# A two-block transformer forward pass on one core: the second attention's order of work rearranged around its recurrent and normalising pieces

## The reference, cut to what matters

```
z   = rms_norm(x, norm_mix) @ w_in
y_a = rg_lru_mixer(...)      # recurrence
y_b = short_conv_mixer(...)  # bg * causal_dwconv(cg * xs, conv_w)
y_c = fox_mixer(...)         # 4 heads of causal attention with a decay
y_d = nsa_mixer(...)         # 4 heads: selected, window and compressed keys, gated
x   = x + concat(rms_norm each) @ w_out
x   = x + (silu(gu[:, :F]) * gu[:, F:]) @ w_down
```

```
r, i  = sigmoid(xc @ w_r + b_r), sigmoid(xc @ w_i + b_i)
log_a = -8 * softplus(-lam) * r
a     = exp(log_a)
b     = sqrt(-expm1(2 * log_a)) * (i * xc)
h[t]  = a[t] * h[t-1] + b[t]
y_a   = h * gelu(gate)
```

## Time and profile before

| what | us |
|---|---|
| median of 3 runs | 774.54 (774.17 to 776.04) |
| the profiled execution, its own time | 776.68 |
| span from its first to its last instruction | 774.9 |
| PE busy | 740.8 (96%) |
| DVE busy | 551.4 (71%) |
| ACT busy | 450.1 (58%) |

### The profile page before, as it was taken

One profiled execution on the slowest core, in us unless ns is written; L12 is line 12 of the kernel. 1 busy time (PEld: TensorE's weight loads), 2 busy tenths in 40 slices (PEclk: granted clock), 3 DMA queues, 4 the chain that ended last, 5 costly groups with the idle time before them and its releaser, 6 DMA issues.

```text
span 774.9 us, 14050 instructions
## 1 busy us (share of the span) xinstructions
PE 740.8 (96%) x4998; PEld 667.2 (86%) x4998; DVE 551.4 (71%) x1064; ACT 450.1 (58%) x855; POOL 63.9 (8%) x94
## 2 busy tenths in 40 slices
PE   3999999999999999999999999979899999999998
PEld 2799888899999899999999998868698888888886
DVE  4886359898897766666666787667776877777674
ACT  5667466665655654554545766378766555554542
POOL 8001020000455000000000002000000000000000
PEclk9799999999999999999999999989999999999999
DMA  8997997888796566665666476422153766666631
GB/s 287 353 265 247 189 239 218 269 265 283 243 311 201 153 201 180 198 189 166 195 188 178 99 207 174 143 82 83 55 163 98 230 202 192 174 188 193 187 108 54
DMA packets 187220, 148.23 MB, mean 191 GB/s; under 512 B 13694, under 2 KB 171328, under 8 KB 187160
## 3 DMA queue, kind: packets, MB, share of 16 engines
q1 hardware_dynamic: 183296, 143.61, 62.8%
q10 hardware_dynamic: 2232, 3.03, 2.2%
q0 software_dynamic: 1648, 1.00, 0.6%
HBM read 146.29 MB, written 1.36 MB: 191 GB/s over the span
## 4 chain that ended last, share of the span: by engine, by line
PE 84%; ACT 5%; DVE 5%; issue 2%; DMA 2%; POOL 0%; SPq 0%; ACTq 0%; DVEq 0%; POOLq 0%
PE ps L2273 20%; PE ps L1886 14%; PE ps L1888 14%; PE ps L1887 14%; PE ps L2275 10%; DMA raw<-in_w_ada 2%; ACT w_hi L707 2%; DVE w_lo L1211 1%; DVE arena L1269 1%; PE ps L2250 1%; PE ps L2366 1%; PE ps L2141 1%; PE ps L1934 1%; PE ps L2163 1%; PE ps L2128 1%
## 5 line engine op out<-in xcount | busy, mean ns | idle before, releaser
L1211 DVE TENSOR_TENSOR w_lo<-raw,w_hi 128x1024 fp32r<-128x1024 f32 (+3 forms) x223 | 269.1, 1228 | 73.9 <-ACT w_hi L707 72.6
L2273 PE MATMUL ps<-h,w_hi 128*128 128x512 f32 x672 | 239.2, 396 | 0.0
L707 ACT ACTIVATE w_hi<-raw 128x1024 fp32r<-128x1024 f32 (+3 forms) x223 | 226.1, 1038 | 21.3 <-PE ps L1888 7.9
L2275 PE MATMUL ps<-h,w_lo 128*128 128x256 f32 x672 | 189.4, 282 | 0.0
L2273 PEld LDWEIGHTS ps<-h,w_hi 128*128 128x128 f32 x672 | 126.3, 188 | 29.6
L1886 PE MATMUL ps<-h,w_hi 128*128 128x256 f32 (+1 forms) x440 | 127.7, 290 | 2.7 <-ACT bias L1102 1.1
L2275 PEld LDWEIGHTS ps<-h,w_lo 128*128 128x128 f32 x672 | 126.2, 188 | 1.0
L1888 PE MATMUL ps<-h,w_lo 128*128 128x256 f32 (+1 forms) x440 | 124.4, 283 | 0.0
L1887 PE MATMUL ps<-h,w_hi 128*128 128x256 f32 (+1 forms) x440 | 124.4, 283 | 0.0
L1886 PEld LDWEIGHTS ps<-h,w_hi 128*128 128x128 f32 (+1 forms) x440 | 83.7, 190 | 7.7 <-issue 5.8
L1887 PEld LDWEIGHTS ps<-h,w_hi 128*128 128x128 f32 (+1 forms) x440 | 83.8, 191 | 0.0
(11 more groups left out here) (372 smaller groups left out, 1273.7 us busy)
## 6 DMA issues: line engine op xcount, KB each, us to landing
raw<-in_w_in SPq DMA_DIRECT2D x53, 512.0 KB, 5.7
raw<-in_w_down SPq DMA_DIRECT2D x44, 512.0 KB, 4.3
raw<-in_w_gate_up SPq DMA_DIRECT2D x44, 512.0 KB, 4.7
raw<-in_w_ada SPq DMA_DIRECT2D x32, 512.0 KB, 4.8
raw<-in_w_gate SPq DMA_DIRECT2D x22, 512.0 KB, 3.9
raw<-in_w_up SPq DMA_DIRECT2D x22, 512.0 KB, 5.1
raw<-in_w_ada SPq DMA_DIRECT2D x32, 256.0 KB, 6.5
raw<-in_w_o SPq DMA_DIRECT2D x8, 512.0 KB, 5.1
```

The costliest lines, as they stand in the source:

```text
L707: A(w_hi[:, m % HL, 0:w], raw[:, n % RAW, 0:w], ACT.Copy).then_inc(hi_done, 1)
L1211: V.tensor_tensor(w_lo[:, m % HL, 0:w], raw[:, n % RAW, 0:w], w_hi[:, m % HL, 0:w].bitcast(f32), sub).then_inc(lo_done, 1)
L2273: T.matmul(bank[:, :], hi, h2[:, k, :, :].rearrange("p a b -> p (a b)"), start=(k == 0), stop=False, skip_group_check=True)
L2275: ins = T.matmul(bank[:, 0:SEQ], lo, h_hi[:, k, :], start=False, stop=(k == KC - 1), skip_group_check=True)
```

## The change

On every engine the same work is done; only its order changes, and ACT needs one change of table less.

1. ACT does `exps` of the first pair before the LRU's `tanh` and `exp`.
2. DVE computes `decay_rates` in feed-forward network 1, after `hidden(2)`, and no longer between the key norms and the first scores.
3. DVE normalises the first pair before it splits the next weight panel; its wait for `gate2_ready` comes after both.
4. DVE's `lru_w` moves from round 5 to round 4, and the two `conv` calls of rounds 5 and 6 move behind the `probabilities` of the same round.
5. ACT's square root for the LRU (`lru_sqrt`) moves from round 6 to round 4, beside `y_root(0)`; the GELU moves from round 5 to after round 7.
6. PE does the compressed key's norm matmul before the LRU's gate matmuls.

```diff
 ACT
-            line.settle()
+            for g in PAIRS[0]:
+                exps(g)
+            act.wait_ge(s("lru_sig"), 4)
             act.wait_ge(s("lru_c"), 1)
             for c in range(2):
                 line(A(yT[:, c, :], ra[:, c, :], ACT.Tanh, scale=spt[7][:, c:c + 1]), "lru_tanh")
             for c in range(2):
                 line(A(ra[:, c, :], ra[:, c, :], ACT.Exp, scale=spt[6][:, c:c + 1]), "lru_a")
-            for g in PAIRS[0]:
-                exps(g)
             fill(EARLY)
...
                 if x == 4:
                     y_root(0)
-                    line(A(warm, eps_c, ACT.Exp))
-                if x == 5:
-                    line(A(lg, lg, ACT.Gelu_apprx_tanh), "lg_ready")
-                    line.settle()
-                    line(A(warm, eps_c, ACT.Exp))
-                if x == 6:
                     act.wait_ge(s("lru_w"), 1)
                     line(A(yT[:, 0:2, :], yT[:, 0:2, :], ACT.Sqrt), "lru_sqrt")
+                    line(A(warm, eps_c, ACT.Exp))
+            line(A(lg, lg, ACT.Gelu_apprx_tanh), "lg_ready")
             act.wait_ge(s("yb_ready"), 1)
             y_square(1)
+            line(A(warm, eps_c, ACT.Sqrt))
             pair_copy(*PAIRS[-1])
             y_root(1)
 DVE
                     hidden(j, 0, [e + 3 * j - 1 + k for k in range(3)])
+                if f == 0:
+                    decay_rates()
                 with dve.Fori(0, ITER) as i:
...
-            decay_rates()
             dve.wait_ge(s("kc_rms"), 1)
...
-            dve.wait_ge(s("gate2_ready"), 1)
             for g in PAIRS[0]:
                 scores(g)
-            split.ahead(nth("fill", EARLY))
             for g in PAIRS[0]:
                 probabilities(g)
+            split.ahead(nth("fill", EARLY))
+            dve.wait_ge(s("gate2_ready"), 1)
             for x, (a, b) in enumerate(PAIRS):
                 if more:
                     scores(a + 2)
                     scores(b + 2)
+                if x == 4:
+                    dve.wait_ge(s("lru_tanh"), 2)
+                    dve.wait_ge(s("lru_a2"), 1)
+                    line(stt(out=yT[:, 0:2, :], in0=xc, scalar=1.0, in1=yT[:, 0:2, :], op0=add, op1=mult), "lru_w")
...
-                if x == 5:
-                    dve.wait_ge(s("lru_tanh"), 2)
-                    dve.wait_ge(s("lru_a2"), 1)
-                    line(stt(out=yT[:, 0:2, :], in0=xc, scalar=1.0, in1=yT[:, 0:2, :], op0=add, op1=mult), "lru_w")
+                if more:
+                    probabilities(a + 2)
+                    probabilities(b + 2)
+                if x == 6:
+                    y_low(0)
                 if x in (5, 6):
...
                     conv(s_c[:, c, :], sx, 3, "sc_conv_w_2", None, c)
-                if more:
-                    probabilities(a + 2)
-                    probabilities(b + 2)
-                if x == 6:
-                    y_low(0)
 PE
+            pe.wait_ge(s("kc_sq"), 1)
+            line(T.matmul(ps[7][:, 304:304 + NCMP], half1[:, :], kcq[:, 0:NCMP], start=True, stop=True), "cmp_mm")
             arrived(pe, "in_lw")
             pe.wait_ge(s("xc_ready"), 2)
             for q in range(4):
...
                 line(T.matmul(lin(l, SEQ, SEQ * c), lw[:, g, c, :], xc[:, c, :], start=True, stop=True), "lru_mm")
-            pe.wait_ge(s("kc_sq"), 1)
-            line(T.matmul(ps[7][:, 304:304 + NCMP], half1[:, :], kcq[:, 0:NCMP], start=True, stop=True), "cmp_mm")
```

More of the change, by code:

```diff
@@ L1103, in _ @@
                        bias=vcol("lru_b_gates_2", q)), "lru_sig")
-            line.settle()
-            act.wait_ge(s("lru_c"), 1)
-            for c in range(2):
-                line(A(yT[:, c, :], ra[:, c, :], ACT.Tanh, scale=spt[7][:, c:c + 1]), "lru_tanh")
-            for c in range(2):
-                line(A(ra[:, c, :], ra[:, c, :], ACT.Exp, scale=spt[6][:, c:c + 1]), "lru_a")
             def y_square(n):
@@ L1130, in _ @@
                 exps(g)
+            act.wait_ge(s("lru_sig"), 4)
+            act.wait_ge(s("lru_c"), 1)
+            for c in range(2):
+                line(A(yT[:, c, :], ra[:, c, :], ACT.Tanh, scale=spt[7][:, c:c + 1]), "lru_tanh")
+            for c in range(2):
+                line(A(ra[:, c, :], ra[:, c, :], ACT.Exp, scale=spt[6][:, c:c + 1]), "lru_a")
             fill(EARLY)
@@ L1501, in _, with decay_rates @@
             modulate(5)
+            def decay_rates():
+                dve.wait_ge(s("lam_exp"), 1)
+                e_, s_, s2, acc_, t_ = spt[0], spt[1], spt[2], spt[3], spt[4]
+                line(V.tensor_scalar(t_, e_, 2.0, None, add))
+                line.settle()
+                line(V.reciprocal(t_, t_))
+                line.settle()
+                line(V.tensor_tensor(s_, e_, t_, mult))
+                line.settle()
+                line(V.tensor_tensor(s2, s_, s_, mult))
+                line(V.memset(acc_, 1.0 / 15))
+                for k in (13, 11, 9, 7, 5, 3, 1):
+                    line.settle()
+                    line(V.tensor_tensor(acc_, acc_, s2, mult))
+                    line.settle()
+                    line(V.tensor_scalar(acc_, acc_, 1.0 / k, None, add))
+                line.settle()
+                line(stt(out=acc_, in0=acc_, scalar=2.0, in1=s_, op0=mult, op1=mult))
+                line.settle()
+                line(V.tensor_scalar(t_, vcol("lru_lambda_2", 0, 2), -1.0, 0.0, mult, ALU.max))
+                line.settle()
+                line(V.tensor_tensor(acc_, acc_, t_, add))
+                line.settle()
+                line(V.tensor_scalar(spt[7], acc_, 8.0, None, mult))
+                line(V.tensor_scalar(spt[6], acc_, -8.0, None, mult), "lru_c")
             def raw_low(c):
```

25 lines of the change are left out of this document (removed).

## The result

The changed kernel takes 769.34 us (median of 5 runs, 768.3 to 771.58), the kernel before 776.04 beside it (5 runs, 774.17 to 777.95): the ratio on record is 0.9933, with an interval of 0.9913 to 0.9953 (the two medians alone would give 0.9914), so it is faster, by less than 1%. The profiled execution took 769.34 us with a span of 767.5, against 776.68 and 774.9.

A forecast was written before the change was run, and what follows sets the result against it. PE, busy 740.8 of 774.9 us, was taken as the bound, leaving its waits and low-clock stretches to win. Terms 5.2 + 0.7 + 0.7 + 0.3 = 6.9 us took the median from 774.54 to 767.6, range 765.4 to 770.8.

The forecast's parts named there:

- rival 1: Whole kernel: the forecast itself holds, 765.6 to 769.3 us; chance 0.72.
- start, up to turn 2: Start of the attention: first waits shrink and the clock stays full, so turn 1 comes 5.2 us earlier.
- rounds, up to turn 6: Rounds 4 to 6: both waits before turn 6 go, round 5's gather wait grows to 1.6; net 0.7 us won.
- round 7, up to the panel: Round 7: 0.7 of PE's 2.4 us of waits go, 1.7 stay.
- behind round 7, to the end: After round 7: 0.3 us won, taken between clock falling as before (nothing won) and clock full (0.7 won).
- "1.85 us": Between turn 0 and turn 1 on PE: 7.15 against 5.30 us, the difference of 1.85 charged to the low clock.
- Rival 2: Start gives half back: the gather's new wait nears 3 us or the clock falls again; 770.1 us, chance 0.13.
- that sign of the prediction: Start of the attention: PE has no wait before the first chunk, the 1.13 us there gone.
- Decay rates: Moved to feed-forward network 1 on DVE: cost 0, its next step 3.5 us late, hidden by a four-panel lead.
- Rival 3: Table loads hold ACT longer than their rows show; one less gives 1.3 us more, 766.3 or lower; chance 0.06.
- Rival 4: Tail: rounds come earlier but PE waits for late y_total(1) and second group's root; 773 to 775 us, chance 0.05.
- Rival 5: First rounds: PE's clock stays at 0.50, up to 5.3 us more per round, kernel slower, 777.5 us; chance 0.04.

The follow-up runs named there:

- e1: Changed kernel with the reordering of rounds 4 to 7 on ACT and DVE undone, only the attention's start kept changed: 771.79 us, 0.9926 of the kernel before.
- e12: Changed kernel with the compressed key's norm matmul back behind the LRU's gate matmuls on PE: 771.05 us, 0.9952 of the kernel before.
- e9: The changed kernel run and profiled again, no edit: 771.83 us, 0.9964 of the kernel before.
- e14: The kernel before, profiled again without edit (second of three repeats): 777.0 us.
- e15: The kernel before, profiled again without edit (third of three repeats): 772.43 us.
- e13: The kernel before, profiled again without edit (first of three repeats): 778.33 us.
- e16: The changed kernel, profiled once more without edit: 771.43 us.
- e2: Kernel before with only the reordering of rounds 4 to 7 applied, the attention's start as before: 775.61 us, 0.9971 of the kernel before.
- e5: Changed kernel with DVE's decay rates back ahead of the key norm, before the first scores: 771.97 us, 0.9944 of the kernel before.
- e6: Changed kernel with DVE's two convolutions back ahead of the probabilities in rounds 5 and 6: 772.16 us, 0.995 of the kernel before.
- e7: Changed kernel with ACT's GELU back in round 5, with its wait and table reload: 770.69 us, 0.9936 of the kernel before.
- e8: Changed kernel with three unread matmuls added on PE where it waits in round 7: 770.89 us, 0.9942 of the kernel before.
- e10: Changed kernel with the LRU's tanh and exp on ACT moved to round 1, behind its splits: 768.72 us, 0.9916 of the kernel before.
- e11: As e10, plus in round 6 DVE does P7's probabilities and y_low(0) before the split: 770.22 us, 0.9942 of the kernel before.
- e3: Changed kernel with ACT's first-pair exponentials back behind the LRU's tanh and exp: 771.61 us, 0.9923 of the kernel before.
- e4: Changed kernel with DVE splitting the next weight panel before normalising the first pair again: 775.21 us, 0.9977 of the kernel before.

## Why the prediction was right, and where it was not

The direction and the mechanism were right. The size was right between the two first profiles, and too large as a statement on the kernels. Over the executions timed beside e1 to e12, the kernel before has a mean of 776.04 us (70 executions); the changed kernel has 771.39 (17, of the result and e9): 4.6 less, not 6.9. That the two first profiles differ by 6.8 is luck: the terms were read from an execution of the kernel before that was dearer than two of the other three, and were compared with the cheapest of three of the changed kernel. The ratio of 6.9 us, 0.9910, lies just beyond the interval of the result, and the median of 769.34 just above the 765.6 to 769.3 of rival 1, though inside the wider range. The forecast of 767.6 also started from a median of 3 runs that lay 1.5 below the mean of the 70.

The table compares the terms with the stretch between the first profiles and with the means of all profiled executions (4 of before, 3 of the changed kernel), each a difference of two columns of the table above:

```
term                         forecast   first profiles   means
start, up to turn 2               5.2             5.15    3.75
rounds, up to turn 6              0.7             0.48    0.48
round 7, up to the panel          0.7             1.22    1.23
behind round 7, to the end        0.3            -0.06   -1.21
sum                               6.9             6.79    4.25
```

The profiles of before are four and lie 5.5 us apart, so the mean of 4.25 has a standard error of about 1.5. Steadier is what lies behind turn 1: to the end it is 257.6 us before and 257.5 after in the mean of the profiles. The gain that holds comes ahead of turn 1.

**Start.** A failed step: the term of 5.2 is too large by some 1.5. It charged "1.85 us" to the clock between turn 0 and turn 1, and took the wait of 4.60 and the root's wait of 1.41 as the kernel's. All three are one execution's. In e14 and e15 the waits are 3.0 and 0.54, that round takes 22.55 - 16.91 = 5.6 us, and turn 1 comes 2.4 earlier than in the first profile: 0.86 through ACT's root, since its matmul stands behind gate matmuls at low clock, and 7.15 - 5.64 = 1.51 through the round at low clock. The other 0.3 of the 1.85 stays at full clock, as the second head's transposes still wait for DVE. The sentence beside it, "this takes the clock to be full there, as the new wait is less than half of the old one", fails as an argument: the clock was full behind 3.0 us of standing still in e14, low behind the same 3.0 us in e13 (there the round takes 28.05 - 20.02 = 8.0 us) and low behind 1.80 in e16. e2 is a second case of low behind 3.0. The length of the wait alone does not decide it. Rival 2 named this cost and gave it to one case in eight; it is present in one of the three profiles of the changed kernel, e16, where turn 1 to turn 2 takes 6.3 us instead of 5.3.

The rest of the walk held. On the clock of the kernel before (0.61 later) turn 0 stands at 503.57, for 503.6; the scores of P1 at 506.63, for 506.7; turn 1 at 510.96, for 510.9; a new wait of 1.65, for 1.7, released by `ptb`, L895. Two things inside it were off. The new wait for the second head (0.3) was not there. And the 1.4 us by which the sigmoids were to come earlier hold only against the first profile, with its gate matmuls at low clock; with these at full clock part 6 is worth 0.5 (e12). The first chunk had no wait in two profiles of three because PE was held up in the gate matmuls by the low clock; in e16, where it was not, 1.03 is left. So that sign of the prediction came true by luck.

**Decay rates.** Cost nothing, as forecast: PE does not wait anywhere in feed-forward network 1. On DVE the first addition behind them stands here,

```profile
278.06 0.41 DVE L1548 TENSOR_TENSOR arena<-arena,ps 128x256 f32<-128x256 f32 x1
```

10.97 us behind its like of the step before (267.09), where it was 7.55 (275.42 behind 267.87): 3.4 later, for 3.5, and well inside the lead of four panels. e5 shows that they did not have to go: in their old place they end 0.3 us ahead of the first scores, in a profile without a loss against e16.

**Rounds 5 to 7.** The wait before the gather of round 5 grew to 1.35, for 1.6, both waits before turn 6 are gone, and 1.06 + 0.67 = 1.7 stay in round 7, for 1.7. Both terms together were 1.4 and are 1.7. In the table the term of round 7 is 1.2 for 0.7; 0.3 of this is the wait of turn 6's second head, which falls behind the start of turn 6. The convolution behind the probabilities is worth 1.4 of the 1.7 by itself (e6 against e5). The GELU's new place is worth 0.3 at turn 7 (e7), and nothing at the end.

**Behind round 7.** The term that failed altogether: 0.3 won was forecast, 1.2 are lost in the mean. Its local working was right: `y_total(1)` is ready 1.1 us ahead of PE, as forecast, in this row of DVE against PE's 550.94;

```profile
549.43 0.43 DVE L1703 TENSOR_TENSOR sq<-sq 128x256 f32<-128x256 f32 x1 [0.19 <-ACT sq L1108]
```

and where the clock stays full PE waits 0.43 to 0.53 for it, for 0.6 (e7, e8). But the forecast's "if the clock falls there as before" took the earlier trace rows as what the kernel before does. In three of its four executions it does not fall there: panel to sums 1 takes 3.47 us, not 5.08. In all three of the changed kernel it does: 5.10, 5.10, 5.02. The prediction's estimate of 3.5 us for this piece at full clock was right; its case was not. So against those three executions the 1.2 us won in round 7 are lost right behind it, and e2 shows the same with the old start (5.10). In e6, e7, e8 and e10 the clock is full there (3.57 to 4.07 us, the waits included), so the low clock is not bound to the changed order; why it falls in three profiles of three stays open. In e8, with the clock full, 1.03 come back behind the panel and 0.45 at the end.

**Rivals.** Rival 2's sum, 770.1, is nearer to the measured 769.34 than the forecast's 767.6, but not by its mechanism in that profile: the new wait is 1.65 and the clock behind it is full. Rival 3 fell: the table load at 499.14 lasts 1.28 us and the exponential starts 1.29 behind its start, with ACT at work right before. The Trainium skill's 2.66 us for a switch ("ScalarE: Activation LUTs", "What ACT_TABLE_LOAD costs") does not agree with this row; the row decides. Rival 4 did not occur: the tail's new waits are 0.4 to 0.5 (e7, e8) where the clock leaves any. e11 shows that the mechanism exists, since there, with the rounds 2.7 us earlier, `y_total(1)` is late by 1.66. Rival 5 did not occur: from 506 to 512 the granted clock is 1.00; in e16 one round is slow, by 1.0 us. None of them named the case that happened: that the first profile of before had dearer waits and low clock in dearer places than two of the next three.

**How sure the smaller gain is.** In the executions timed beside each other the time follows what the clock cost: per microsecond of (1 - granted clock) times the time, 0.52 us within each kernel, with a standard error of 0.06. The kernel before has 7.7 us of it in the mean, the changed kernel 5.9. Worked out at equal clock the gain is 3.7 us, with 0.9 either way; for e10 it is 6.0, against the same 70 executions. PE's waits up to the first panel, summed as in the prediction, are 10.3 us in the first profile of before, 9.4, 8.0 and 8.0 in e13 to e15, and 4.7, 4.7 and 6.1 in the three of the changed kernel: 3.8 less in the mean. The gain thus lies at 4.6 by the timed runs, 4.25 by the profiles and 3.7 at equal clock; which of these is nearest stays open, and so does what decides where the clock falls.

## What to carry to other kernels

Before a stretch of low clock is booked as the price of a wait, look at several executions of the same kernel: here four of one kernel differed by 5.5 us in the same stretch, and the forecast rested on a dearer one. Price waits by what stands behind them: a wait with another wait behind it is worth little of its length (e3: 0.15 of 1.05). A slow stretch ahead of a wait of the same engine costs nothing (the first chunk of e14) unless another engine waits for what is made in it (the gate matmuls of the first profile, 0.86 through ACT's root). And the length of a wait can itself come from the clock: 1.41 and 0.54 are the same wait of the same kernel. The strongest edit of this change was the plainest: the engine that others wait for does the work that is ready before it waits for a producer (e4), and the same rule, applied to the LRU's `tanh` and `exp`, took away the wait that the change had left (e10).

## What the runs showed of the hardware

The granted clock was 0.50 while PE was busy for 2.00 of 2 us, in the LRU's gate matmuls of the changed kernel's profile (496 to 498) and in the first chunk of e14 (504 to 506), and it was 1.00 in the same gate matmuls of e16. In e9 the low stretch around the gate matmuls was longer, and everything behind came 1.4 us later than in the first profile (turn 0 at 13.77, for 12.38). The places differ between executions of one kernel, and the wait just ahead does not fix them: the clock was full behind 3.0 us without work in e14 and low behind 3.0 in e13. The Trainium skill ("TensorE: Matmul & The Clock Gate", Part 1) says that the chip's watch over PE's work is not tied to the kernel's start, so that one kernel shows different numbers of slow matmuls in different runs. The repeats here agree with that. Its remark that the slow start is under 1% of a typical kernel's time speaks of the start; here the slow stretches lie deep in the kernel, and their places make repeats of the kernel before differ by 5.5 us, 0.7% of its time, more than the change of 0.6% is worth.
